# Mixer A probabilities of sample tiles: 32x32 block transpose on VectorE and a block exchange by DMA through DRAM, in place of transposes on TensorE

## The reference, cut to what matters

```
s = einsum('bqhcd,bshcd->bhcqs', qb, k) * scale        # c = 0, 1
p = softmax(s, axis=-1)
p = p[:, :, 0] - lam[None, :, None, None] * p[:, :, 1]
out = einsum('bhqs,bshe->bqhe', p, v)                   # 128 queries at a time
```

## Time and profile before

| | |
|---|---|
| three runs | 1254.29 us median (1253.92 to 1254.44) |
| profiled execution | span 1253.5 us from its first to its last instruction; of this execution the profile gives the span alone |
| granted TensorE clock | 0.997 of full speed on average, 1.00 in each stretch of mixer A looked at |
| heads of mixer A, 512 to 1072 us | PE busy all the time, DVE 327 us, ACT 330 us, POOL 140 us of 560 us |

### The profile page before, as it was taken

How to read it: one execution, slowest core, us unless ns; L and a number is a source line. 1 busy time by engine, 2 the same in 40 slices (tenths; PEclk the granted TensorE clock), 3 DMA queues, 4 the chain that set the end, 5 groups by cost and what they waited for, 6 DMA issues and landing times.

```text
span 1253.5 us, 16906 instructions
## 1 busy us (share of the span) xinstructions
PE 1222.7 (98%) x6251; PEld 991.3 (79%) x6251; DVE 800.0 (64%) x1242; ACT 619.1 (49%) x1296; POOL 258.3 (21%) x439
## 2 busy tenths in 40 slices
PE   5899999999999999999999999999999999999996
PEld 3455778888888888888888888888888888888885
DVE  4455488667586776755546374554647675789774
ACT  5522325645555465565556555656556765312223
POOL 1211033012031040222221221222223322211111
PEclk9999999999999999999999999999999999999998
DMA  9999242222221232322222121222224423756544
GB/s 348 371 377 349 84 110 76 62 71 74 76 96 44 67 106 53 100 60 83 71 61 86 51 91 51 82 59 83 59 72 133 139 83 98 254 187 228 184 135 177
DMA packets 130482, 156.45 MB, mean 125 GB/s; under 512 B 8304, under 2 KB 97040, under 8 KB 129632
## 3 DMA queue, kind: packets, MB, share of 16 engines
q1 hardware_dynamic: 116528, 109.60, 26.7%
q0 software_dynamic: 13424, 45.20, 11.4%
q10 hardware_dynamic: 448, 0.57, 0.1%
HBM read 144.18 MB, written 11.16 MB: 124 GB/s over the span
## 4 chain that ended last, share of the span: by engine, by line
PE 92%; SPq 3%; DVE 2%; DMA 1%; ACT 1%; POOL 1%; issue 0%; POOLq 0%; DVEq 0%; ACTq 0%
PE z_ps L704 24%; PE z_ps L706 23%; PE z_ps L705 23%; PE ring L795 5%; PE ring L884 4%; SPq L658 2%; PE ring L829 2%; PE ring L828 2%; PE ring L730 2%; PE ring L888 2%; DMA ada_raw<-in_w_ada_dram 1%; PE ring L706 1%; PE ring L705 1%; PE ring L891 1%; PE ring L704 1%
## 5 line engine op out<-in xcount | busy, mean ns | idle before, releaser
L704 PE MATMUL z_ps<-w_hi,xt_hi 128*128 128x512 f32 x1350 | 554.1, 410 | 2.6 <-issue 1.1
L706 PE MATMUL z_ps<-w_hi,xt_lo 128*128 128x512 f32 x1350 | 527.7, 391 | 0.0
L705 PE MATMUL z_ps<-w_lo,xt_hi 128*128 128x512 f32 x1350 | 527.2, 391 | 0.0
L1007 ACT ACTIVATE w_hi<-w_raw 128x512 fp32r<-128x512 f32 x270 | 169.3, 628 | 334.9 <-PE z_ps L706 309.2
L704 PEld LDWEIGHTS z_ps<-w_hi,xt_hi 128*128 128x128 f32 x1350 | 254.0, 188 | 68.1 <-issue 27.2
L1441 DVE TENSOR_TENSOR w_lo<-w_raw,w_hi 128x512 fp32r<-128x512 f32 x270 | 196.8, 732 | 162.6 <-ACT w_hi L1007 162.2
L706 PEld LDWEIGHTS z_ps<-w_hi,xt_lo 128*128 128x128 f32 x1350 | 253.4, 188 | 55.3
L705 PEld LDWEIGHTS z_ps<-w_lo,xt_hi 128*128 128x128 f32 x1350 | 254.8, 189 | 38.8
L1542 DVE TENSOR_REDUCE small<-s_sb 128x2 f32<-128x1536 f32 (+1 forms) x60 | 87.6, 1460 | 20.6 <-ACT s_sb L1007 20.6
L1153 ACT ACTIVATE s_sb<-s_sb,small 128x768 f32<-128x768 f32 (+1 forms) x120 | 98.0, 821 | 3.6 <-DVE small L1542 3.5
L1902 POOL TENSOR_TENSOR sg<-sg,zs 128x128 f32<-128x128 f32 (+1 forms) x60 | 38.6, 644 | 276.2 <-DVE sg L1511 275.6
(11 more groups left out here) (196 smaller groups left out, 1378.3 us busy)
## 6 DMA issues: line engine op xcount, KB each, us to landing
w_raw<-in_w_in_dram SPq DMA_DIRECT2D x188, 256.0 KB, 3.1
ada_raw<-in_w_ada_dram SPq DMA_DIRECT2D x64, 512.0 KB, 11.6
w_raw<-in_w_out_dram SPq DMA_DIRECT2D x64, 256.0 KB, 3.8
gate_raw<-in_w_ada_dram POOLq DMA_DIRECT2D x12, 1024.0 KB, 8.0
w_raw<-in_w_in_dram POOLq DMA_DIRECT2D x20, 256.0 KB, 6.3
o_spill<-row_st POOLq DMA_DIRECT2D x14, 320.0 KB, 3.4
row_st<-o_spill POOLq DMA_DIRECT2D x14, 320.0 KB, 3.3
x_sb<-in_x_sample_dram SPq DMA_DIRECT2D x4, 1024.0 KB, 9.6
```

The source lines that it names most:

```text
L704: pe.matmul(out, hi_l, hi_r, start=start, stop=False)
L705: pe.matmul(out, hi_l, lo_r, start=False, stop=False)
L706: return pe.matmul(out, lo_l, hi_r, start=False, stop=stop)
L1007: return act.activation(out, in_, ACT.Copy, **kw)
```

## The change

The probabilities of sample tiles (t = 1 to 4) of mixer A are no longer transposed by TensorE.

- ScalarE writes the scores to `s_sb` in another order of keys (`quads`: the keys of a 128-block are split in four groups of 32, and the group is the outermost index). The part with the cached keys is now two copies instead of one.
- VectorE, after it has combined the halves, transposes every 32x32 block in place of its partition group (L1619 of the changed kernel) and writes with a step of six elements, so that the six key blocks of one query lie side by side. The result overwrites the second half of `s_sb`.
- SyncE sends it to a DRAM tensor `p_blocks` by four DMAs (32 partitions each, rows of 192 elements), which puts every block in the right group of partitions, waits for them, and loads it back to `pt_t` (one DMA of 128x768). Both are issued in `turn_blocks`, behind the weight loads that are due by then.
- TensorE's `step_t` has nothing to do for these tiles, and its six products of `step_v` wait for `pt_t` and take their stationary operand from it with a step of six elements (24 bytes): `pt_t[t % 2][:, :, j]` instead of `pt_f[:, keys]`.
- ScalarE's copies to `pt_f` go, but for tile 0. New waits keep buffers apart: ScalarE's score copies wait until the DMAs have read the buffer (`p_out`), the second DMA waits for the V step two tiles before.

```diff
@@ banks_of
     if kind == "T":
-        return (2 if t else 1) * (2 if g == "G" and t else 1)
+        return 0 if t and g == "D" else 4 if t else 1
@@ build
+    p_blocks = nc.dram_tensor("p_blocks", (2, P, NKEY), F32).ap()
...
-    pt_f, _ = place("pt_f", [P, NKEY], F32, pt0)
+    QUAD, KB = 4, LAT + PAST
+    pt_t = [place(f"pt_t{i}", [P, P, KB], F32, pt0 + 4 * NKEY * i)[0] for i in range(2)]
+    pt_f, _ = place("pt_f", [P, P], F32, pt0 + 4 * NKEY * 2)
...
+        def quads(row):
+
+            return row.rearrange("p (i k b) -> p k i b", i=QUAD, b=P // QUAD)
@@ SyncE
+            def turn_blocks(a, t):
+
+                b, n = t % 2, p_count(a, t)
+                sp.wait_ge(p_turned, (TILES - 1) * (a - D_IT) + t)
+                if n > 1:
+                    sp.wait_ge(pt_in[b], 16 * (n - 1))
+                for j in range(QUAD):
+                    rows = slice(P // QUAD * j, P // QUAD * (j + 1))
+                    src = s_sb[rows, b, 1, :].rearrange("a (i n) -> a i n", i=QUAD)
+                    dst = p_blocks[b].rearrange("(i a) (j n) -> j a i n", i=QUAD, j=QUAD)[j]
+                    sp.dma_start(dst, src).then_inc(p_out[b], 16)
+                sp.wait_ge(p_out[b], 16 * QUAD * n)
+                if t > 2:
+                    wait_full(sp, TURN[("V", a, t - 2)])
+                else:
+                    wait_full(sp, TURN[("V", a - 1, t + 2 if group_kind(a - 1) == "D" else TILES - 1)])
+                sp.dma_start(pt_t[b][:, :, :].rearrange("p q k -> p (q k)"), p_blocks[b]).then_inc(pt_in[b], 16)
+
+            j = EARLY_PAIRS
+            for q, (it, s) in enumerate(ORDER):
+                turns = [(a, t) for kind, a, t in (steps_at(*ORDER[q - 1]) if q else []) if kind == "S" and t and group_kind(a) == "D"]
+                if turns:
+                    while j <= min(q // 2 + 3, len(ORDER) // 2 - 1):
+                        load_w(sp, j)
+                        j += 1
+                for a, t in turns:
+                    turn_blocks(a, t)
+            for j in range(j, ITS * KT // 2):
                 load_w(sp, j)
@@ TensorE, step_v
+                if t and group_kind(a) == "D":
+                    pe.wait_ge(pt_in[t % 2], 16 * p_count(a, t))
...
-                        ins = pe.matmul(bank[:, 0:DH], pt_f[:, keys], v_f[:, vt, :],
+                        ins = pe.matmul(bank[:, 0:DH], pt_t[t % 2][:, :, j] if t else pt_f[:, :], v_f[:, vt, :],
@@ ScalarE, scores_out
+                    if t > 2:
+                        act.wait_ge(p_out[t % 2], 16 * QUAD * p_count(a, t - 2))
+                    elif t == 1 and a > D_IT:
+                        act.wait_ge(p_out[1], 16 * QUAD * p_count(a - 1, 3))
                     for c_ in range(2):
                         wait_full(act, n + c_)
+                        copy(quads(s_sb[:, t % 2, c_, :])[:, 0:LAT], RB(n + c_)[:, :].rearrange("p (k i b) -> p k i b", k=LAT, i=QUAD),
                              scale=DK_A ** -0.5).then_inc(free_sem(n + c_), 1)
...
@@ VectorE, combine
                 dve.scalar_tensor_tensor(e1, e2, fac[:, b, 0:1], e1, ALU.mult, ALU.add).then_inc(p_ready, 1)
+                if t:
+                    dve.wait_ge(p_ready, m + 1)
+                    dve.transpose(e2.rearrange("p (i b k) -> p i k b", i=QUAD, k=KB), e1.rearrange("p (i k b) -> p i k b", i=QUAD, k=KB)).then_inc(p_turned, 1)
```

More of the change, by code:

```diff
@@ L434, in build @@
         pt_hi_done = sem("pt_hi_done")
+        p_turned = sem("p_turned")
+        p_out, pt_in = ([sem(f"{w}{b}") for b in range(2)] for w in ("p_out", "pt_in"))
         o_part, o_sq, o_rstd, og_ready = sem("o_part"), sem("o_sq"), sem("o_rstd"), sem("og_ready")
@@ L537, in t_parts, with p_count @@
                 return [(n, c, 0, 1, P * c, c == heads(a) - 1) for c in hs]
+            if group_kind(a) == "D":
+                return []
             return [(n + 2 * c + j // 4, c, j, m, 0, True) for c in hs for j, m in ((0, 4), (4, 2))]
+        def p_count(a, t):
+            return 2 * (a - D_IT) + (t - 1) // 2 + 1
+        def quads(row):
+            return row.rearrange("p (i k b) -> p k i b", i=QUAD, b=P // QUAD)
         PT_BEFORE = {}
@@ L673, in _ @@
                 load_ada(n)
-            for j in range(EARLY_PAIRS, ITS * KT // 2):
+            def turn_blocks(a, t):
[24 more added lines that the diff above has]
+            for j in range(j, ITS * KT // 2):
                 load_w(sp, j)
@@ L1127, in scores_out @@
                     act.wait_ge(zr_ready, a + 1)
-                if group_kind(a) == "D":
+                if group_kind(a) == "D" and t == 0:
+                    if a > D_IT:
+                        act.wait_ge(p_out[0], 16 * QUAD * p_count(a - 1, 4))
                     for c_ in range(2):
                         wait_full(act, n + c_)
-                        kn = 512 if t else P
-                        copy(s_sb[:, t % 2, c_, 0:kn], RB(n + c_)[:, 0:kn],
+                        copy(s_sb[:, 0, c_, 0:P], RB(n + c_)[:, 0:P],
                              scale=DK_A ** -0.5).then_inc(free_sem(n + c_), 1)
-                    if t:
-                        wait_full(act, n + 2)
-                        copy(s_sb[:, t % 2, :, 512:NKEY], RB(n + 2)[:, :].rearrange("p (c k) -> p c k", c=2),
-                             scale=DK_A ** -0.5).then_inc(free_sem(n + 2), 1)
+                    return
+                if group_kind(a) == "D":
+                    if t > 2:
+                        act.wait_ge(p_out[t % 2], 16 * QUAD * p_count(a, t - 2))
+                    elif t == 1 and a > D_IT:
+                        act.wait_ge(p_out[1], 16 * QUAD * p_count(a - 1, 3))
+                    for c_ in range(2):
+                        wait_full(act, n + c_)
+                        copy(quads(s_sb[:, t % 2, c_, :])[:, 0:LAT], RB(n + c_)[:, :].rearrange("p (k i b) -> p k i b", k=LAT, i=QUAD),
+                             scale=DK_A ** -0.5).then_inc(free_sem(n + c_), 1)
+                    wait_full(act, n + 2)
+                    for c_ in range(2):
+                        ins = copy(quads(s_sb[:, t % 2, c_, :])[:, LAT:],
+                                   RB(n + 2)[:, 256 * c_:256 * (c_ + 1)].rearrange("p (k i b) -> p k i b", k=PAST, i=QUAD),
+                                   scale=DK_A ** -0.5)
+                    ins.then_inc(free_sem(n + 2), 1)
                     return
```

## The result

The changed kernel takes 1285.39 us (median of 4 runs, 1283.3 to 1286.43), the kernel before 1254.37 (1253.92 to 1254.48). The ratio is 1.0248 with a 95% interval of 1.0233 to 1.0262: slower, and above the range. I had forecast 1238. The profiled execution spans 1284.4 us, against 1253.5 of the earlier trace rows.

The account below looks back on a forecast made before the run. TensorE's own stream was taken to bound mixer A's heads. Terms of -21.8 + 0 + 1.4 + 3.8 = -16.6 us gave about 1238 us; the forecast's own range was 1233 to 1248, the full range reached 1275.

Parts of the forecast that it names:

- What the products cost with strided weights: V's weight loads from columns 24 bytes apart on TensorE: taken as 0, with 39 us as the other end.
- slower loads: Rival: each strided weight load of V takes a second streaming time, 0.107 us more; 1273 us in all, chance 0.30.
- Transposes leave TensorE: Six transposes per sample tile leave TensorE in mixer A's heads, 0.68 us for each of 32 tiles: -21.8 us.
- Waits of tile 4 in seven heads: V of tile 4 waits 0.2 us for its blocks in each of seven heads: 1.4 us.
- The trip of 7.4 us: Stores to DRAM and load back, from transposed probabilities to pt_t: 7.4 us, low end 6.5, high end 11.6.
- The last head's wait: V of tile 4 in the last head waits 3.8 us once for its blocks, part of it already at tile 3.
- the 2.71 us of idle time before L1550 cover it: VectorE's new transpose, 1.1 us a tile with its wait, is hidden by VectorE's idle time in each such step.
- Late blocks: Rival: the trip through DRAM takes 11.6 us in every head, 34 us more, giving 1272 us; chance 0.08.

Follow-up runs that it names:

- e5_before_strided: The kernel before, with ScalarE writing pt_f in interleaved order and V's six products reading it with a step of six elements; 1293.94 us, ratio 1.0315.
- e13_six_heads: Kernel before, but heads 5 to 10 use the DMA way with unstepped transpose, ScalarE's copy in runs of 32 and tile 4's V later; 1238.16 us.
- e3_both: The changed kernel with V's operand taken from adjacent columns and the loads of x_add and gate_b one step earlier; 1249.63 us, ratio 0.996.
- e2_operands_early: The changed kernel with GpSimd's loads of x_add and gate_b one step earlier in the last head; 1282.46 us, ratio 1.0227.
- e8_compact_pool: The changed kernel with x_add and gate_b loaded a step earlier and GpSimd copying pt_t to adjacent columns for V; 1304.73 us, ratio 1.0396.
- e7_compact_act: The changed kernel with x_add and gate_b loaded a step earlier and ScalarE copying pt_t to adjacent columns for V; 1268.75 us, ratio 1.0112.

## Why the prediction was wrong

**Failed, and decided the sign: "What the products cost with strided weights", where I took 0.** The step costs 1.22 us a tile, 39 us in all (39.9 by e5_before_strided alone). The bounds were right: I had worked out 38 to 41 us for a second streaming time as the far end. The choice between the ends was wrong. I had gone by "the row of the same kind nearest to it", L730, two columns 64 bytes apart. A load of two columns lasts 84 ns in either layout; it can't show a price of about 1 ns a column (125 ns over 128 columns). Two columns had about 2 ns of it to show, inside the spread of 81 to 87 ns in the earlier trace rows. That a row says nothing about a cost is not the same as its saying that there is none. On the other side stood a load whose streaming part was as long as the pair, with no slack, and a rule that named the case. The chance of 0.30 for "slower loads" was too small for that.

**The rival had the mechanism and the size of its main term.** Its V was "about 2.55 us" (measured 2.57) and its loads "about 300 ns" (317). It gave 1273; the 12 us missing are waits and half clock in and behind the last two heads.

**Transposes leave TensorE, -21.8 us: right**, shown by e13_six_heads. (2.05 - 2 x 0.68 is 0.69 and not 0.68, 0.3 us over all tiles.)

**Waits of tile 4 in seven heads, 1.4 us: none in the changed kernel, for another reason than I gave.** V itself took 1.22 us longer each time, which puts the V of tile 4 later, and none waits. Where V has its old length, in e3_both, tile 4 waits 0.9 us in one middle head (640.89) and in no other. So the seven waits of 0.2 us were not there as I had them. The transpose on VectorE took 1.63 and not 1.0 us. I had priced it by the combination of the same size and named twice 1.02 as the upper bound "if the strided write halves its rate". The write did cost; it is the same error as with the loads, a second time. Without the step it takes 0.98 us, the value I had used.

**The trip of 7.4 us: 1.2 us too long in the middle heads.** From the end of the transpose (640.4) to the load's landing (643.64 + 3.0) it was 6.2 us, below my low end of 6.5. The stores land in 1.9 us (median), where I took 2.5, and at most in 8.5.

**The last head's wait, 3.8 us: too small.** It was 7.3 us, with 1.8 us of half clock behind it. I had named the meeting with `x_add`, but not priced it, and took the middle heads' landing times there. In the profile of e2_operands_early 5 of the 7.3 us went with this meeting, in the median 2.9 us of time. The clock came down behind this wait, so it cost more than its own length; I had no term for that.

**Head 11, 3.3 us: "the 2.71 us of idle time before L1550 cover it" failed there.** I had let VectorE's idle time hide the transpose. In head 11 the reciprocal behind the transpose starts 1.6 us later against the combination than before, and by GpSimd and `row_st` ScalarE's score copies come late for V's bank, as the rows of the result show. No experiment took this chain apart; e13_six_heads shows only that the waits of both heads go when these heads keep the old way. Why L837 and L966 wait for VectorE (1.3 us each) stays open too.

**"Late blocks" in every head: did not happen**, as I thought: in the changed kernel no V waits for its blocks but that of tile 3 in the last head.

## What to carry to other kernels

When a change hands TensorE's weight load a stepped operand, look first at whether the load has room to grow. Here it had almost none, and 0.8 of every nanosecond showed. Then price the step by a row of the same length, or keep it as an open term at its bound; a short instruction of the same kind is no evidence. A data path that is to take work off the busiest engine should deliver in the order in which that engine reads; the reordering belongs on another engine, in runs that don't skip. And look at each place where the new path meets other work: an instruction put into an idle engine's program also delays what stands behind it there, for whoever waits for that. Converting six of eight heads gave 16 us here, converting all eight gave 6.

## What the runs showed of the hardware

A weight load of 128 fp32 columns takes 192 ns at a step of 4 bytes, 196 at 8, 261 at 12, and 318 to 329 at 16, 20 and 24 bytes. A start 8 bytes further on changes nothing. V of a tile, 12 loads and matmuls, takes 1.35, 1.42, 2.03 and 2.59 to 2.69 us at these steps.

At a step of 24 bytes 768 fp32 elements per partition take 1.63 us as a write of VectorE's transpose, 1.64 as a read of ScalarE and 1.63 as a read of GpSimd. In adjacent order it is 0.98 on VectorE, in runs of 32 it is 0.84 on ScalarE; GpSimd has no such row. An operation of VectorE on 128x128 beside GpSimd's copy took 1.48 us at 623.78 in e8_compact_pool, and the same one 0.35 at 619.67 in e7_compact_act.

Stores of 96 KB landed in 1.9 us in the middle heads (median), and one in 8.5 us beside 1.8 MB that another queue had just issued. A quarter of the load of 384 KB, in packets of 128 bytes, landed in 2.7 us, the whole in 3.0 (medians).

Behind a wait of 7.3 us TensorE's granted clock was 0.50 from 1088 to 1093.2 us, and 1.00 again from 1096.
